# Products whose sums nobody reads, placed in TensorE's waits around two attentions

## The reference

```python
# first block, layer 2: sparse attention, 12 heads in 2 groups, 4 blocks c of 128 queries
s = einsum(qb, k_cmp) * scale;  p_cmp = masked_softmax(s, cmp_end <= t)      # 31 compressed keys
o_cmp = einsum(p_cmp, v_cmp)
s = einsum(qb, kg) * scale;     p = masked_softmax(s, smask); o_slc = einsum(p, vg)   # selected blocks
s = einsum(qb, kw) * scale;     p = masked_softmax(s, wmask); o_win = einsum(p, vw)   # window of 512
o = o_cmp * gb[..., 0:1] + o_slc * gb[..., 1:2] + o_win * gb[..., 2:3]       # gates: sigmoid(...)
mix = concatenate([o, memory_attention(qm, mk, mv)])                         # 4 memory heads, 256 keys

# second block: sliding-window attention, 8 heads in 2 groups, window 128, a sink per head
s = where(mask, einsum(qb, kc) * scale, -inf)        # a block of 128 queries reads its own and the previous keys
m = maximum(max(s), sink); pexp = exp(s - m)
o = einsum(pexp / (sum(pexp) + exp(sink - m)), vc)
```

## Time and profile before

| | us |
|---|---|
| median of 3 runs | 3653.13 |
| lowest, highest | 3644.2, 3659.81 |
| profiled execution | 3662.95 |
| its span (first to last instruction) | 3661.1 |
| PE busy (19739 products and transposes) | 3438.3 |
| VectorE busy | 1874.9 |
| GpSimd busy | 1681.9 |
| ScalarE busy | 748.9 |

### The profile page before, as it was taken

How to read it: one execution, slowest core, us unless ns; L and a number is a source line. 1 busy time by engine, 2 the same in 40 slices (tenths; PEclk the granted TensorE clock), 3 DMA queues, 4 the chain that set the end, 5 groups by cost and what they waited for, 6 DMA issues and landing times.

```text
span 3661.1 us, 46242 instructions
## 1 busy us (share of the span) xinstructions
PE 3438.3 (94%) x19739; PEld 2709.0 (74%) x19739; DVE 1874.9 (51%) x2862; ACT 748.9 (20%) x1635; POOL 1681.9 (46%) x550
## 2 busy tenths in 40 slices
PE   6989999989999999999999988799999998889998
PEld 5757888886668887778878667678887775668886
DVE  2344445536755446544482465664437667653333
ACT  2242111225531111100102522110002224220001
POOL 4414565870035645666655001456555520636552
PEclk9999999997899999999999878999999999999999
DMA  4112333330013433343223000422223533413221
GB/s 146 61 33 69 132 110 127 106 121 13 1 35 103 138 115 104 109 138 97 94 81 110 29 2 14 138 98 92 93 100 136 203 105 127 155 53 104 92 93 46
DMA packets 253677, 340.75 MB, mean 93 GB/s; under 512 B 9760, under 2 KB 186144, under 8 KB 250912
## 3 DMA queue, kind: packets, MB, share of 16 engines
q1 hardware_dynamic: 230960, 301.51, 25.1%
q10 hardware_dynamic: 22512, 36.28, 2.8%
HBM read 308.15 MB, written 25.43 MB: 91 GB/s over the span
## 4 chain that ended last, share of the span: by engine, by line
PE 82%; DVE 10%; ACT 3%; POOL 2%; issue 1%; DMA 1%; ACTq 0%; DVEq 0%; SPq 0%; POOLq 0%
PE bank L113 80%; PE bank L116 2%; DVE scr L136 1%; DVE al L146 1%; POOL wlo L136 1%; POOL raw L142 1%; ACT ah L131 1%; DVE scr L146 1%; DVE rb L136 1%; DVE st L151 1%; ACT L131 0%; DVE yl L136 0%; DVE x L136 0%; DMA raw<-in_b_w_in 0%; POOL whi L143 0%
## 5 line engine op out<-in xcount | busy, mean ns | idle before, releaser
L143 POOL TENSOR_SCALAR whi<-raw 128x2048 fp32r<-128x2048 f32 x241 | 485.5, 2014 | 1888.2 <-PE bank L113 1179.6
L136 POOL TENSOR_TENSOR wlo<-raw,whi 128x2048 fp32r<-128x2048 f32 x241 | 1137.6, 4720 | 20.1
L113 PE MATMUL bank<-ah,whi 128*128 128x512 f32 x2408 | 963.2, 400 | 44.9 <-DVE al L136 22.9
L113 PE MATMUL bank<-ah,wlo 128*128 128x512 f32 x2408 | 954.7, 396 | 0.0
L113 PE MATMUL bank<-al,whi 128*128 128x512 f32 x2408 | 947.6, 397 | 0.0
L113 PEld LDWEIGHTS bank<-ah,whi 128*128 128x128 f32 x2408 | 454.0, 189 | 171.3 <-issue 25.7
L113 PEld LDWEIGHTS bank<-ah,wlo 128*128 128x128 f32 x2408 | 453.9, 189 | 111.0
L113 PEld LDWEIGHTS bank<-al,whi 128*128 128x128 f32 x2408 | 454.0, 189 | 110.2 <-issue 1.2
L113 PE MATMUL bank<-hh,whi 128*128 128x512 f32 x1040 | 412.5, 397 | 0.0
L113 PE MATMUL bank<-hl,whi 128*128 128x512 f32 x1040 | 410.8, 395 | 0.0
L113 PE MATMUL bank<-hh,wlo 128*128 128x512 f32 x1040 | 410.7, 395 | 0.0
(11 more groups left out here) (426 smaller groups left out, 4200.3 us busy)
## 6 DMA issues: line engine op xcount, KB each, us to landing
raw<-in_w_in SPq DMA_DIRECT2D x34, 1024.0 KB, 5.2
raw<-in_w_mlp_in SPq DMA_DIRECT2D x32, 1024.0 KB, 5.6
raw<-in_w_mlp_out SPq DMA_DIRECT2D x32, 1024.0 KB, 6.3
raw<-in_w_ada SPq DMA_DIRECT2D x24, 1024.0 KB, 5.8
raw<-in_ffn_w_gate SPq DMA_DIRECT2D x22, 1024.0 KB, 5.3
raw<-in_ffn_w_up SPq DMA_DIRECT2D x22, 1024.0 KB, 5.3
raw<-in_ffn_w_down SPq DMA_DIRECT2D x22, 1024.0 KB, 5.0
raw<-in_w_ffn_in SPq DMA_DIRECT2D x22, 1024.0 KB, 5.0
```

The costliest lines, as they stand in the source:

```text
L113: return self.eng.matmul(out, lhsT, rhs, start=start, stop=stop, skip_group_check=True)
L136: return IDLE if self.eng is None else self.eng.tensor_tensor(out, a, b, op)
L143: return self.eng.tensor_scalar(out, a, s1, s2, op0, op1)
```

## The change

A helper `stream` does `n` products of the identity `identR` with the whole constant tile `self.rounded` (512 columns) into a given bank, each as a sum of its own. No instruction reads these sums; the bank is one that TensorE has just taken and overwrites next. The helper is called in three kinds of places:
- in `nsa_pe`, 24 products behind the wait for the gates' bank and before the wait for ScalarE's sigmoid;
- in `attention_pe`, at step 0, behind the waits for the banks and before the waits of `ready`, which stood first until now: 4 products in the sparse attention, 6 in the sliding-window attention;
- in `attention_pe`, between a step's scores and its transposes, behind the wait for the transposes' bank: 8 at step 2 in both attentions, and 2 at each of steps 3, 6, ..., 69 of the sparse one.

The memory attention of the first layer calls `attention_pe` without them. No other engine's list changes.

```diff
--- before.py
+++ after.py
@@ -690,10 +690,14 @@
         t = T["st"][:, i // 2 % self.NSM, :, :]
         return [t[:, c, i % 2:i % 2 + n] for c in range(4)]
 
-    def attention_pe(self, e, name, units, T, ready):
+    def stream(self, e, bank, n):
+
+        for _ in range(n):
+            e.mm(bank[:, :], self.identR, self.rounded[:, :], True, True)
+
+    def attention_pe(self, e, name, units, T, ready, streams={}):
+
         P = self.P
-        for r in ready:
-            e.wait_ge(*r)
         for s in range(len(units) // 2 + 3):
             pair = [(i, units[i]) for i in (2 * s, 2 * s + 1) if i < len(units)]
             banks = []
@@ -701,6 +705,10 @@
                 bank, free = self.ps.take(name, "s", i)
                 e.wait_ge(*free)
                 banks.append(bank)
+            if s == 0:
+                self.stream(e, banks[0], streams.get(0, 0))
+                for r in ready:
+                    e.wait_ge(*r)
             for (i, u), bank in zip(pair, banks):
                 t = e.mm(bank[:, 0:u["nk"]], u["q"], u["k"], True, not u["masks"])
                 if not u["masks"]:
@@ -715,6 +723,8 @@
                     p, nk = T["p"][i % self.NP], units[i]["nk"]
                     bank, free = self.ps.take(name, "turned", i)
                     e.wait_ge(*free)
+                    if i % 2 == 0:
+                        self.stream(e, bank, streams.get(s, 0))
                     e.wait_ge(*self.D.at(name, "p", i))
                     for j in range(-(-nk // 128)):
                         w = min(128, nk - 128 * j)
@@ -1632,13 +1642,16 @@
         self.headnorm_pe(e, "q0", self.query_half(0)[1], 4, 8)
         bank, free = self.ps.take("bgate", "turned")
         e.wait_ge(*free)
+        self.stream(e, bank, 24)
         e.wait_ge(*C.at("bgate", "sigmoid"))
         for t in range(4):
             i = e.tr(bank[:, 128 * t:128 * t + 128], self.gf[:, 128 * t:128 * t + 128], self.ident)
         i.then_inc(*P.up("bgate", "turned"))
         self.headnorm_pe(e, "q1", self.query_half(1)[1], 4, 8)
         self.barrier(e, P, "bq")
-        self.attention_pe(e, "nsa", self.nsa_units(), self.nsa_at, [C.at("q1", "turned", 3)])
+
+        streams = {0: 4, 2: 8, **{s: 2 for s in range(3, 72, 3)}}
+        self.attention_pe(e, "nsa", self.nsa_units(), self.nsa_at, [C.at("q1", "turned", 3)], streams)
         self.lin(e, "out1", A["w_out"][1], 0, 8, [128 * n for n in range(8)], self.xact,
                  lambda k: D.at("nsa", "o", k))
         P.mark("used", "out1")
@@ -1888,8 +1901,7 @@
                  ahead=self.load_constants)
         P.mark("used", "mix2")
         self.barrier(e, P, "mix2 in")
-        self.attention_pe(e, "swa", self.swa_units(), self.swa_at,
-                          [C.at("swk", "turned", 1)])
+        self.attention_pe(e, "swa", self.swa_units(), self.swa_at, [C.at("swk", "turned", 1)], {0: 6, 2: 8})
         self.barrier(e, P, "swa")
         wkv = WkvPe(self, e)
         self.rwkv_order(wkv)
```

## The result

The changed kernel takes 3631.44 us (median of 5 runs, 3629.37 to 3633.47), the kernel before 3653.13 us (median of 5 runs beside it, 3644.2 to 3659.81). The ratio is 0.9942 with a 95% interval of 0.9928 to 0.9957: faster by 0.6%. The forecast was 3625 us with a range of 3612 to 3645. The profiled execution of the changed kernel took 3633.47 us, 29.5 us less than that of the kernel before; the sum had said 31.2 us.

The account below looks back on a forecast made before the run. The chain ran through TensorE for 82% of the span, with low-clock stretches in two attentions. Gains of 22.4 and 10.2 us less costs of 1.2 and 0.2 gave 31.2, less 3: 28 us below the median, 3625 us (3612 to 3645).

Parts of the forecast that it names:

- the sum: Whole kernel: 22.4 - 1.2 + 10.2 - 0.2 = 31.2 us gained if the clock holds everywhere.
- The clock is what is won: Sparse and sliding-window attention: filler products keep TensorE's clock at 1.00, winning 22.4 us and 10.2 us before costs.
- Pairs at full clock take 27.7 us, the eighth step 2.3 us: Sparse attention: a pair of heads falls from 30.78 to 27.7 us, its eighth step from 3.79 to 2.3 us.
- Steps five to nine of pair one: Sparse attention, first pair of heads: these steps take 9.8 us instead of 15.24 us, a gain of 5.4 us.
- Pairs three to six give 12.3 us: Sparse attention: four pairs of heads taking 123.12 us would take 27.7 us each, a gain of 12.3 us.
- the doubt on the stretch in the sliding-window attention: Its 30.72 us low stretch was supposed to end sooner in other executions, so 3 us came off the gain.
- The opening gives 1.0 us and the eight products cost nothing: Sparse attention's start: 0.5 us from transposes, 0.5 us from early scores; the third step's wait hides its eight products.
- 0.1 us at each of twelve places: Every third step of the sparse attention: two products overrun the wait at twelve places, costing 1.2 us in all.
- The sliding-window attention gives 10.2 us: Steps four to eleven fall from 28.48 to 18.4 us, winning 10.1 us; the third step gives 0.1 us.
- the first: Attention steps: the clock still falls in part, low stretches moving to other steps; gain 15 to 22 us, about 3635; 20%.
- The second: Sparse attention's opening stays at low clock, as transposes may not count as activity; about 3634 us; 8%.
- Slower: Attention steps: PE, not the softmax, is the path, so 72 products add 17 to 31 us; 3670 to 3684; 5%.

Follow-up runs that it names:

- u_thirds4: Four products instead of two in each third step of the sparse attention, against the changed kernel; 3641.8 us (one run).

## Why the prediction was right, point by point

- *The clock is what is won.* Right, and shown by parts. The pairs behind the first have 1.00 in all eight profiles with products or transposes in each third step, and lost it in two pairs where every second was left out; the sliding-window attention falls from 50 to 56 us (four profiles without its products) to 40.3 or 40.4 us (all ten with them).
- *Pairs at full clock take 27.7 us, the eighth step 2.3 us.* Right: the eighth step measures 2.26 us. Steps five to nine of pair one take 9.8 us as summed.
- *Pairs three to six give 12.3 us.* Between the two profiles they do (11.5 us with the products' cost). Against the median this is the mis-sized term: the second profile of the kernel before has these pairs at full clock already, so the term runs from 0 to 12 us by the execution. I had put the doubt on the stretch in the sliding-window attention, which turned out to be there every time, and allowed 3 us; the median gained 21.7 us where the profiles differ by 29.5 us, so 8 us was due. How often the pairs run at full clock was seen in four profiles only, so the size of this term in the median is not shown.
- *The opening gives 1.0 us and the eight products cost nothing.* Wrong. The first four steps took 6.98 us and now take 8.59 us, and the first scores come 0.6 us later after the gates: 2.2 us lost, 3.2 us off the sum. Two covers failed. The four products at the first step ran at the low level (1.88 us) and ended 0.7 us behind ScalarE's last query copy (833.15), which was to hide them. For the eight, the wait taken to be the softmax's is the bank's, which they stand behind; they start at 836.63, and at full clock (8 x 0.233 us) they would still end 0.7 us behind VectorE, which has the probabilities scaled at 837.8. At the low level they end 2.1 us behind it. In the kernel before the bank is free before the slow scores end, and the earlier trace rows names VectorE there; the fourth step in the earlier trace rows does name ScalarE's exponential, which frees the bank.
- *0.1 us at each of twelve places.* Right in sum (0.2 us a pair), not in place: the fourth step pays 0.28 us for the bank's wait, the seventh nothing, since its bank is free at once and VectorE is what ends last there; the second step is 0.07 us shorter.
- *The sliding-window attention gives 10.2 us.* 10.0 us in steps four to eleven, and 1.4 us more in the first three steps, whose scores at full clock I had counted at 0.1 us.
- *The sum.* That the two profiles differ by 29.5 us, so near its 31.2 us, is in part luck. It has 3.2 us too much at the opening and 1.4 us too little in the sliding-window attention, and outside the edited stages 3.1 us won and 3.3 us lost cancel.
- *The rivals.* Of the first, one low stretch of 3.4 us in pair one is left, and none elsewhere in the pairs or the memory heads. The second came true only in its first half: the transposes of the opening ran low, but pair one's later steps did not. Its reason, that transposes do not count, is not borne out: the clock fell in the idle time ahead of them. The Trainium skill, "TensorE: Matmul & The Clock Gate", section "Part 4: PE-mode transpose", says that transposes do not count as activity for the clock as other products do. Two profiles here speak against it: twenty transposes kept the full clock with 0.34 us of idle before them, and four transposes in each third step kept pairs at 27.83 us. "Slower" is refuted at two products; u_thirds4 shows its mechanism at four.
- *Not foreseen:* the stage behind the sliding-window attention took 254.6 to 260.6 us over the fourteen profiles with nothing changed in it, and in twelve of them 258.4 us or more; the 257.3 us of the changed kernel is a low one. What sets it was not tried.

## What to carry to other kernels

Where TensorE waits in short steps, profile the kernel twice before pricing its low stretches: one execution may have them all and the next none, and the gain is against the median. Put filler in front of the wait that really ends last; behind it (here the wait for the bank) it is paid but for what a later wait still covers. Begin with one product and look at the clock, since in the one profile taken here one did what two did.

## What the runs showed of the hardware

- The same program lost the clock in four pairs of heads in one execution (123.12 us) and in none of them in another (110.77 us).
- A stretch in which PE is busy 29.22 of 30.72 us can run at 1.2 GHz from end to end, and the same steps with 14 products at their opening run at 2.4 GHz throughout.
- An idle of 3.1 us behind 24 products lost the level; one of 0.34 us behind 36 did not.
- Twenty transposes behind that idle of 0.34 us ran at 2.4 GHz (sixteen of them in 1.91 us; 3.62 us at 1.2 GHz).
